# Groups of seven in fewer column pairs of the down-projections

## The reference

```python
# first block: D_FF = 5632
z = rmsnorm(h, norm_ffn_g[l])
ff = (jax.nn.silu(z @ w_ffn_gate[l]) * (z @ w_ffn_up[l])) @ w_ffn_down[l]
h = h + ff.astype(h.dtype)
return rmsnorm(h, norm_final_g)
...
# second block: D_FF_2 = 8192; its input is the result above, first normed again by g_mix
x = x + jnp.square(jax.nn.relu(hm @ w_up[l])) @ w_down[l]
return rmsnorm_2(x, g_final)
```

## Time and profile before

| | |
|---|---|
| median of 3 runs | 2544.18 us (2543.91 to 2544.43) |
| the profiled execution | 2543.78 us |
| its span | 2542.0 us |
| PE busy | 2506.1 us (99%), 11847 matmuls |
| DVE busy | 1918.2 us (75%) |
| ACT busy | 1359.4 us (53%) |
| GpSimd busy | 407.1 us (16%) |
| HBM read | 478.86 MB, 190 GB/s over the span |

### The profile page before, as it was taken

How to read it: one execution, slowest core, us unless ns; L and a number is a source line. 1 busy time by engine, 2 the same in 40 slices (tenths; PEclk the granted TensorE clock), 3 DMA queues, 4 the chain that set the end, 5 groups by cost and what they waited for, 6 DMA issues and landing times. The chain is left out here.

```text
span 2542.0 us, 33034 instructions
## 1 busy us (share of the span) xinstructions
PE 2506.1 (99%) x11847; PEld 2103.3 (83%) x11847; DVE 1918.2 (75%) x2210; ACT 1359.4 (53%) x1819; POOL 407.1 (16%) x299
## 2 busy tenths in 40 slices
PE   9999999999999999999989999999999999999997
PEld 7889888888888888888779988888888888888886
DVE  5556554655789999999876766565679899989997
ACT  5445454444555555555555554455556655665564
POOL 1001100113112300221112301031132101220121
PEclk9999999999999999999999999999999999999999
DMA  7645556565756566656646655465566666556664
GB/s 240 201 144 157 165 173 191 190 238 178 229 190 202 189 196 233 217 187 200 216 154 182 182 150 159 147 218 171 162 216 199 198 215 205 186 196 211 203 221 138
DMA packets 252755, 485.99 MB, mean 191 GB/s; under 512 B 15339, under 2 KB 38844, under 8 KB 251468
## 3 DMA queue, kind: packets, MB, share of 16 engines
q1 hardware_dynamic: 248604, 463.99, 57.0%
q0 software_dynamic: 3696, 20.00, 2.1%
q10 hardware_dynamic: 320, 0.20, 0.0%
HBM read 478.86 MB, written 5.27 MB: 190 GB/s over the span
## 5 line engine op out<-in xcount | busy, mean ns | idle before, releaser
L2022 DVE TENSOR_TENSOR w_lo<-w_raw,w_hi 128x1024 fp32r<-128x1024 f32 (+6 forms) x554 | 673.3, 1225 | 419.0 <-ACT w_hi L1381 414.9
L1666 PE MATMUL acc<-w_hi,xT_hi 128*128 128x512 f32 (+4 forms) x2020 | 783.3, 388 | 2.4 <-DVE xT_lo L2132 1.8
L1666 PE MATMUL acc<-w_lo,xT_hi 128*128 128x512 f32 (+4 forms) x2020 | 772.0, 382 | 0.0
L1666 PE MATMUL acc<-w_hi,xT_lo 128*128 128x512 f32 (+4 forms) x2020 | 771.4, 382 | 0.0
L1381 ACT ACTIVATE w_hi<-w_raw 128x1024 fp32r<-128x1024 f32 (+6 forms) x554 | 557.3, 1015 | 400.1 <-PE acc L1666 377.2
L1666 PEld LDWEIGHTS acc<-w_hi,xT_hi 128*128 128x128 f32 x2020 | 379.5, 188 | 71.3 <-issue 3.0
L1666 PEld LDWEIGHTS acc<-w_lo,xT_hi 128*128 128x128 f32 x2020 | 379.1, 188 | 69.8
L1666 PEld LDWEIGHTS acc<-w_hi,xT_lo 128*128 128x128 f32 x2020 | 379.7, 188 | 66.2 <-issue 0.5
L2053 DVE TENSOR_TENSOR w_lo<-w_raw,w_hi 128x1024 fp32r<-128x1024 f32 (+1 forms) x204 | 294.7, 1482 | 39.3 <-ACT w_hi L1410 37.7
L1410 ACT ACTIVATE w_hi<-w_raw 128x1024 fp32r<-128x1024 f32 (+1 forms) x204 | 200.6, 1018 | 108.5 <-PE acc L1666 99.9
L1666 PE MATMUL acc<-w_hi,hT_hi 128*128 128x512 f32 x568 | 222.9, 392 | 1.7 <-DVE w_lo L2022 1.7
(11 more groups left out here) (506 smaller groups left out, 3601.8 us busy)
## 6 DMA issues: line engine op xcount, KB each, us to landing
w_raw<-in_w_in SPq DMA_DIRECT2D x168, 512.0 KB, 3.6
w_raw<-in_w_down SPq DMA_DIRECT2D x102, 512.0 KB, 4.2
w_raw<-in_w_up SPq DMA_DIRECT2D x100, 512.0 KB, 4.3
w_raw<-in_w_ffn_down SPq DMA_DIRECT2D x72, 512.0 KB, 4.3
w_raw<-in_w_ffn_gate SPq DMA_DIRECT2D x68, 512.0 KB, 4.3
w_raw<-in_w_ffn_up SPq DMA_DIRECT2D x68, 512.0 KB, 3.8
w_raw<-in_w_out SPq DMA_DIRECT2D x64, 512.0 KB, 4.0
s_raw<-in_w_up SPq DMA_DIRECT2D x28, 512.0 KB, 5.7
```

The lines of the kernel that those rows point to most:

```text
L1666: ins = pe.matmul(ac[t][:, 0:n], a[:, l0 + c, t * P:(t + 1) * P], w[:, slot, c, 0:n], start=start and c == 0 and m == 0, stop=stop and c = ...
L2022: dve.tensor_tensor(w_lo[:, slot, 0:kc, 0:n], w_raw[:, slot, 0:kc, 0:n], w_hi[:, slot, 0:kc, 0:n].bitcast(F32), ALU.subtract).then_inc(lo_ ...
```

## The change

Three tables of plans are written anew, and with them the code that lays them out:

- `DOWN`, the 24-chunk pieces (three of them): four sevens in each pair, where the second pair had five, and another order in the second pair.
- `REST_GLU`, the 20-chunk piece: three sevens in the first pair as before, none in the second (it had two). The second pair becomes two plain blocks, one after the other.
- `REST_RELU`, the 16-chunk piece: two sevens in the first pair as before with two plain tiles exchanged, none in the second (it had three).
- The turns of the last hidden features stand behind other tiles: `glu6`, `relu6` and `relu4` behind number 4 (was 1 or 2), `relu5` and `relu3` behind number 3 (was 1), `glu5` behind number 4 (was 1); in the last piece `relu4` behind number 3 (was 2).
- `u0`, `u1`, `u2` are turned behind tiles number 2, 4 and 6 of the fourth block of the 20-chunk piece.

The input sums are made for as many sevens as the larger pair of the piece has: 4 instead of 5, 3 as before, 2 instead of 3.

```diff
@@ -87,9 +87,9 @@
     return dict(n=n, plans=plans, home=home, ring=ring, sums=sums)
 
 
-DOWN = sevens((4, 5), ("00101101S01S01S01S01", "0010S10S10S10S11S01"), ring=((1, 3), (1, 3)), sums="dve")
-REST_GLU = sevens((3, 2), ("00101101S01S01S01", "001011S0101S001011"), home=FAR, ring=((1,), (1,)), sums="dve")
-REST_RELU = sevens((2, 3), ("00101101S01S01", "01S10S00S0"), home=FAR, ring=((1,), (1,)), sums="dve")
+DOWN = sevens((4, 4), ("00101101S01S01S01S01", "0010S101S010S10S1101"), ring=((1, 3), (1, 3)), sums="dve")
+REST_GLU = sevens((3,), ("00101101S01S01S01",), home=FAR, ring=((1,),), sums="dve")
+REST_RELU = sevens((2,), ("00110101S01S01",), home=FAR, ring=((1,),), sums="dve")
 
 FETCHES = (0, 1, 2, 3, 4, 5, 8, 6, 7, 9, 10, 11, 12, 13, 14, 15)
 
@@ -256,7 +256,7 @@
     return [("tile", b, k) for k in range(tiles_in(b))] + [("evac", b, (0, 1))]
 
 
-def block_pair(w, k0, kc, c0, needs, turn, plan, group, between={}, held=0):
+def block_pair(w, k0, kc, c0, needs, turn, plan, group, between={}):
 
 
     b = [make_block(w, k0, kc, c0 + 512 * j, 512, "hT", 0, "add", c0 + 512 * j, needs, turn) for j in range(2)]
@@ -282,8 +282,8 @@
             part += 1
         if k[j] == len(plain):
             out.append(("evac", b[j], (0, 1)))
-    assert k == [len(plain), len(plain) - held] and q == group["n"], (plan, k, q)
-    return out, [("shared", c0, p, group) for p in range(part, 4)], b[1], plain[k[1]:]
+    assert k == [len(plain)] * 2 and q == group["n"], (plan, k, q)
+    return out, [("shared", c0, p, group) for p in range(part, 4)]
 
 
 def both(name):
@@ -398,8 +398,8 @@
 
         needs = (None,) * (6 - len(last)) + last
         g = [group_of(DOWN, half, turn, 24) for half in range(2)]
-        one, rest, _, _ = block_pair(w, k0, 24, 0, needs, turn, DOWN["plans"][0], g[0], {1 + i: both(x) for i, x in enumerate(last)})
-        two, left_over, _, _ = block_pair(w, k0, 24, 1024, (), turn, DOWN["plans"][1], g[1], {1 + i: [x] for i, x in enumerate(rest)})
+        one, rest = block_pair(w, k0, 24, 0, needs, turn, DOWN["plans"][0], g[0], {4 - i: both(x) for i, x in enumerate(last[::-1])})
+        two, left_over = block_pair(w, k0, 24, 1024, (), turn, DOWN["plans"][1], g[1], {1 + i: [x] for i, x in enumerate(rest)})
         return with_sums(one, g[0], units) + two + left_over + [("sums_back",)] * more
 
     gate = lambda j, needs=(): ("w_ffn_gate", 0, DC, 512 * j, 512, "xT", 0, "silu", 0, needs)
@@ -408,12 +408,12 @@
     S += [("x_sums",)] + weave(up(0), [[], [("angles",)], [], [], [("x_split",)]], 1) + [("swiglu_up", 0, 6)]
     S += down("w_ffn_down", 0, 0, 4, True, "glu6")
     S += [("swiglu_up", 5, 6, "apart"), ("gain", 3), ("gain", 4)]
-    g = [group_of(REST_GLU, half, 4, 20) for half in range(2)]
-    one, rest, _, _ = block_pair("w_ffn_down", 24, 20, 0, hidden_needs("glu5", 5), 4, REST_GLU["plans"][0], g[0], {1: both("glu5")})
+    g = group_of(REST_GLU, 0, 4, 20)
     norms = [pieces_of_norm(3, j) for j in range(4)]
-    two, _, _, _ = block_pair("w_ffn_down", 24, 20, 1024, (), 4, REST_GLU["plans"][1], g[1],
-                              {0: rest[:1], 1: rest[1:] + norms[0], 4: norms[1], 13: both("u0"), 14: norms[2] + both("u1")})
-    S += with_sums(one, g[0], 2) + two + norms[3] + both("u2")
+    one, rest = block_pair("w_ffn_down", 24, 20, 0, hidden_needs("glu5", 5), 4, REST_GLU["plans"][0], g, {4: both("glu5")})
+    S += with_sums(one, g, 2)
+    for j, placed in ((2, {0: rest[:1], 1: rest[1:] + norms[0], 4: norms[1]}), (3, {2: both("u0"), 4: both("u1"), 6: both("u2")})):
+        S += after_tiles(block_steps("w_ffn_down", 24, 20, 512 * j, 512, "hT", 0, "add", 512 * j, (), 4), placed) + norms[j]
 
     w = lambda c0, n, evac, arg=0: block_steps("w_in_2", 0, DC, c0, n, "xT", 0, evac, arg)
     S += out_of_norm(3, make_block("w_in_2", 0, DC, IN2_CQ, 416, "xT", 0, "c", 0, U_NEEDS))
@@ -474,16 +474,17 @@
     S += [("relu2_up", 0, 6)] + down("w_down_2", 0, 0, 0, True, "relu5", "relu6")
     S += [("relu2_up", 4, 8, "apart")] + down("w_down_2", 24, 8, 0, True, "relu3", "relu4")
     S += [("relu2_up", 10, 6, "apart"), ("gain", 7)]
-    g = [group_of(REST_RELU, half, 8, 16) for half in range(2)]
+    g = group_of(REST_RELU, 0, 8, 16)
     norms = [pieces_of_norm(7, j) for j in range(3)]
-    one, rest, _, _ = block_pair("w_down_2", 48, 16, 0, (None, None, "relu3", "relu4"), 8, REST_RELU["plans"][0], g[0],
-                                 {1: both("relu3"), 2: both("relu4")})
-    two, rest_two, last, held = block_pair("w_down_2", 48, 16, 1024, (), 8, REST_RELU["plans"][1], g[1],
-                                           {0: rest[:1], 1: rest[1:] + norms[0], 3: norms[1]}, LEAD)
-    S += with_sums(one, g[0], 0) + two + rest_two + norms[2]
-
+    one, rest = block_pair("w_down_2", 48, 16, 0, (None, None, "relu3", "relu4"), 8, REST_RELU["plans"][0], g,
+                           {1: both("relu3"), 3: both("relu4")})
+    S += with_sums(one, g, 0)
+    S += after_tiles(block_steps("w_down_2", 48, 16, 1024, 512, "hT", 0, "add", 1024, (), 8),
+                     {0: rest[:1], 1: rest[1:] + norms[0], 3: norms[1]}) + norms[2]
+    last = make_block("w_down_2", 48, 16, 1536, 512, "hT", 0, "add", 1536, (), 8)
+    S += [("tile", last, k) for k in range(8 - LEAD)]
     for t in range(NT):
-        S += [("part", last, k, t) for k in held]
+        S += [("part", last, k, t) for k in range(8 - LEAD, 8)]
         S += [("evac", last, (t,)), ("ssq", 7, 3, t), ("rstd", 7, t)]
         S += [s for j in (0, 2, 1, 3) for s in (("scaled", 7, j, t), ("store", 7, j, t))]
     return number(S)
```

## The result

The changed kernel took 2528.07 us (median of 4 runs, 2527.55 to 2529.65) beside 2544.30 us of the kernel before (4 runs, 2543.91 to 2546.47): 0.9937 of it, 95% interval 0.9921 to 0.9953, so 16.2 us less. The forecast was 2532.2 us. Run again later, beside 15 runs of the kernel before, the changed kernel took 2527.47, the ratio again 0.9937 (0.9924 to 0.9951).

The account below looks back on a forecast made before the run. The prediction took PE's stream of 512-column matmuls as the bound. Its terms summed to -11.95 us against the profiled 2543.78, giving 2531.8; with 0.4 for the median of runs, 2532.2 us, range 2528.6 to 2537.0.

Parts of the forecast that it names:

- (a): 20-chunk second pair: PE waits for b_sum_far_hi, then runs at a lowered clock; 7.40 us lost, expected to go.
- (c): Leaving the 20-chunk projection: the transpose of u starts late; 2.44 us lost, expected to go.
- `glu5`, -1.8: Start of 20-chunk first pair: later transposes leave one 2.6 us wait for w_lo, gaining 1.8 us; bounds -0.1 and -2.5.
- the first rival: 20-chunk start: the clock falls again at glu5, adding 1.75 us, giving 2533.9 us; chance 0.16.
- (d): 16-chunk second pair: seven waits for shared_far, w_lo and b_sum_far_lo; 6.10 us lost, expected to go.
- The end, -1.25: Kernel end: without shared sums token tile 0 finishes earlier, so the last addition into x_sb starts 1.25 us sooner.
- Turns, -1.5: 24-chunk projections: moving transposes behind tiles 4 and 5 clears two waits for hT_lo, gaining some 1.5 us.
- first sevens, +2.9: Three 24-chunk projections: b_sum_lo comes about 1.0 us late for each first seven, costing 2.9 us; bounds 0 and 6.
- no new waits: 24-chunk projections: the first sevens' new waits do not come, 2.9 us less, giving 2529.3 us; chance 0.15.
- Five places matter: Claim that PE's losses lie at two 20-chunk pairs, that projection's exit, the 16-chunk second pair and the kernel's end.
- only PE's work counts: Whole kernel: waits are paid back later and only the added matmuls remain, slower at 2549.6 us; chance 0.05.
- ACT's queue: Plain stretches: norm squares ahead of w_hi hold ACT, costing 7 x 2.44 = 17.1 us, slower at 2549.3; chance 0.05.

Follow-up runs that it names:

- before_pinned: Kernel before plus one GpSimd wait: in the relu loops the first group's b_sum starts only after VectorE's split of the tile ahead; 2538.43 us, ratio 0.9982.
- again: The kernel before, run once more with no edit; 2541.64 us, ratio 1.0000.
- glu5 later: Kernel before with only the glu5 transposes moved from behind tile 2 to behind tile 5 of the 20-chunk first pair; 2543.01 us, ratio 1.0001.
- after again: The changed kernel, run once more with no edit; 2527.47 us, ratio 0.9937 of the kernel before.
- early turns: Changed kernel with the turns of the 24-chunk pieces back at their old places behind the first tiles; 2526.50 us, ratio 0.9939 of the kernel before.
- late sums: Changed kernel with GpSimd's input sums of the 20-chunk piece held back by two tiles; 2527.00 us, ratio 0.9938 of the kernel before.

## Why the prediction was right in kind and short in size

By its own steps, with the profiles of before and after:

1. *24 more matmuls, +5.44*: exact. PE had no cover for them; the 24-chunk pieces lose 0.0 us behind their first seven with either plan.
2. *(a) gone, -7.40*, and 3. *(c) gone, -2.44*: sum -9.84; the stretch went from 10.1 to 0.3, -9.8. No plain tile waits for `w_lo` behind a norm piece.
4. *`glu5`, -1.8*: the stops are 0.84 + 1.55 us and, with their slow restarts, the start of the piece loses 3.0 instead of 4.65, -1.65. The forecast's one wait of 2.6 us for `w_lo` came as two, and I had the first of them wrong: it is for the bank `acc` of the third tile, which I took to run without a stop since its `w_lo` exists. The sum came out near 2.6 all the same, since the second stop ends with DVE's `w_lo`, whatever the first took: 10.92 us after the first matmul of the piece, where the forecast has 1221.94 - 1211.09 = 10.85. The clock stayed up in every profile with the later `glu5`, so the first rival falls. But my ground for it, that the clock stays up after 2.28 us idle, does not hold: in four other profiles it fell after that very wait (last section).
5. *(d) gone, -6.10, +0.2*: the piece went from 6.3 to 0.2, -6.1.
6. *The end, -1.25*: from the last matmul's start to the end of the span it was 9.92 us (2542.0 - 2532.08) and is 8.62 (2526.1 - 2517.48), -1.30.
7. *Turns, -1.5, and first sevens, +2.9*: measured -2.2 and +2.8. The chain of splits summed over eight pieces held to 0.1 us in each piece, and the rival "no new waits" falls. The term for the turns was too small by 0.7, since I took idle times from the list for two places and left out the slow restart behind them.
8. *Nothing elsewhere in the 24-chunk pieces*: right.

**What failed is the sentence "Five places matter".** PE lost 4.7 us in the relu loops behind the second and third 24-chunk pieces, in waits for `hT_lo` and `b_sum_lo`, and I gave them no term, since the change does not touch their code. In the changed kernel they lose 1.2 and 2.0. With the order of GpSimd and DVE fixed there in both kernels, the change is worth 2538.43 - 2525.52 = 12.9 us, beside 11.95 summed; the turns' 0.7 is most of what lies between them, but so small a difference is within the scatter of these runs (the two profiled executions differ by 11.6, with the clock up at `glu5` in `before_pinned`). Without it, in the same series, it is 2543.18 - 2527.47 = 15.7. The 2.8 between is, by the medians, what the change got from the loops; the profiles of before and after put it at 3.5. So the term that was missing is the loops' 3.5 us, and the turns' 0.7 makes up nearly all the rest of the 4 us by which the forecast fell short.

Why the loops lose less after the change is only in part known. The immediate cause is shown: GpSimd's `b_sum` starts at a landing load, DVE's split at PE's pace, and they meet or miss each other by tenths. The meeting differs by profile and not by plan alone. With the old plan of the 24-chunk pieces the relu loops lost 4.7, 5.0 and 4.8 us (before, again, glu5 later), also 4.8 with the later turns alone, but 3.9 and 3.0 with only the 16-chunk or only the 20-chunk part changed, which stand behind and ahead of them. With the new plan of these pieces they lost 3.3 alone, and 1.2, 2.0, 2.1 and 3.2 with the whole change (after, after again, early turns, late sums). So the loops lose less with the change in most profiles, but with one or two profiles of each kernel no run shows which part of the change does it. What sets the moment at which the load lands was not tested, and stays open.

The rival that only PE's work counts, with the page "Perfetto Trace Analysis" of the Trainium skill ("Identifying the Most-Contended Engine") beside it, falls plainly: 24 matmuls were added to the engine that is busy 99%, and the time fell by 0.63%. So does the rival by ACT's queue.

## What to carry to other kernels

List every place where the bounding engine misses its pace, over the whole span, and not only in the code that changes: places that lose by a near meeting of two engines can change from one execution to the next. Where such a meeting costs the bounding engine, fix its order with one semaphore wait before measuring anything else; it was worth 4.75 us here for one line, and the runs scattered less with it. A group of operations that saves work on the bounding engine is worth it only where the engines that prepare it are free ahead of it: cost its first member by the chain of splits, which could be summed to 0.1 us here.
